# First-pair quads 0, 2, 3, 5 with one made ahead, and the residuals of the MLPs added by transfers

## The chip, the cores and the metric

The kernel runs on one core of one Trainium2 chip. The time is the device time of one execution in microseconds (us), median of three runs. It was 2813.29 us before the change (2812.1 to 2817.95).

## The reference, cut to what matters

Two transformer-like blocks follow each other on x, 256 tokens by 2048 channels, in float32. Each block has a normalisation, a wide input projection, three mixing branches with gates, an output projection added to x, and an MLP. The branches don't matter here. The MLP does:

```
x = x + merged @ w_out[l]
h2 = rmsnorm(x, norm2_g[l])
x = x + jnp.square(jax.nn.relu(h2 @ w_mlp_in[l])) @ w_mlp_out[l]      # 2048 -> 8192 -> 2048
```

The second block has the same with `w_o_2`, `w_up_2` and `w_down_2`; a last normalisation with `final_g` follows.

## The kernel before, in words

**Products in float32 from three products.** Every weight tile and every activation is split into a high part, rounded to float32r, and a low part, the rest. A product is high by high, high by low and low by high: three matmuls (`three`, L868). ScalarE makes the high part of a weight unit (`cut`, L1136) and VectorE the low one (L1609).

**Units.** The work of TensorE is one list of 2230 units. A plain unit is a weight tile of 256 rows by 512 columns, 512 KB, and both halves of 128 tokens: 12 matmuls. All engines walk the same list. SP loads unit u into one of four buffers when unit u - 4 has been split (L784). ScalarE and VectorE split unit u + 2 when they stand at u (AHEAD = 2), and the split buffers are four deep too. Beside the units, each engine has tasks, tied to a unit by `at(task, unit)`: an engine that stands at unit u first splits unit u + 2 and then does the tasks of u, in the order in which they were put there. An engine works strictly in that order, so a task that waits holds up all behind it.

**An MLP.** The 8192 hidden channels are made in eight groups of 1024. Group 0 is two plain blocks of eight units. Groups 1 to 7 are pairs: two blocks of 512 columns whose units alternate, eight quads of two units each. A quad is 2 x 2 tiles of weights by 2 x 2 tiles of activations, plainly 24 matmuls. For some quads seven products of sums of tiles stand in for eight (`pair_unit`, L873): 21 matmuls, for which VectorE makes three sums of weight tiles (L1622, L1624, L1626; four sums in all), ScalarE their high parts in two instructions (L1142, L1144) and VectorE their low parts in two (L1633). `SEVEN_I` (0, 1, 2, 3, 5, 6) are these quads in the six later pairs of each MLP, `FIRST_I` (1, 3, 5, 6) in the first. Quads 0 and 2 of the later pairs are made ahead: SP loads their weights once more into a tile of their own (L767), and the sums are made during the block before the pair (`ahead_sum`, `ahead_hi`, `ahead_lo`). The first pair has none made ahead. The sums of the activations (`x_sums`) are made during group 0.

**Second matrix.** After pair j come the four column blocks of group j - 1 with the second matrix, ("o1", j - 1, c) or ("o2", j - 1, c): four plain units each, 192 matmuls for the four. PSUM has two accumulator slots of two banks; block b uses slot b % 2. When a column block ends, VectorE adds it to X out of PSUM (`residual`, L2121) in the task ("ev", "o1") at the block's last unit, and that frees the slot. A pair takes both slots: its first quad needs the second one free in its second unit.

**Turning the hidden tile.** The hidden tile is transposed on VectorE (L2094), moved by four small transfers on SP's queue (L758), and split on ScalarE (L1408) and VectorE (L2115).

In the order of tasks at one unit, ("ev", "o1") stands ahead of `ahead_hi`, because it was put there first. GpSimd has hardly any work and issues no transfer.

Of the kernel before, what the change touches and what calls it, by code (L numbers as in the profile page):

```python
# [12 lines left out]
P = 128  # L13
# [32 lines left out]
def build(nc, a, out):  # L46
    ctx = ExitStack()

    def sem(name):
        return ctx.enter_context(nc.semaphore(name))  # L50
# [71 lines left out]

    NAMES = list(B)
    SEVEN_I = (0, 1, 2, 3, 5, 6)
    FIRST_I = (1, 3, 5, 6)
    MADE_AHEAD = (0, 2)
    SETS = ("T", "Y", "H", "T", "Y", "H")
    NI = len(SEVEN_I)
# [19 lines left out]
    for n in range(14):  # L148
        u0 = min(u for u in PAIR if PAIR[u][0] == n)
        js = FIRST_I if n % 7 == 0 else SEVEN_I  # L150
        ahead = () if n % 7 == 0 else MADE_AHEAD
        order = [i for i in js if i in ahead] + [i for i in js if i not in ahead]
        for k, i in enumerate(js):
            buf = ("TY"[k % 2] if n % 7 == 0 else SETS[k]) + str(n // 7 + 1)
            key = buf if buf[0] == "T" else (buf, n)
            rec = Seven(n, i, SEVEN_I.index(i), k == 0, k == len(js) - 1, i in ahead, buf, u0 + 2 * i, USED.get(key), made + order.index(i))
            USED[key] = u0 + 2 * i + 1
            SEVEN[u0 + 2 * i], SEVEN[u0 + 2 * i + 1] = (rec, 0), (rec, 1)
            if i in ahead:
                AHEAD_OF[n, ahead.index(i)] = rec  # L160
        PAIR_END[n] = u0 + 2 * js[-1] + 1
        made += len(js)
# [56 lines left out]
    zc_prod, cc_tap, vc_done = sem("cc_product"), sem("cc_tap"), sem("cc_out")  # L219
    pool_hi = sem("pool_hi")  # L220
    xs, xs_hi, xs_lo, diag, rsb = sem("x_sums"), sem("x_sums_hi"), sem("x_sums_lo"), sem("root_diagonal"), sem("root_rows")
    t_sum, t_hi, t_lo = sem("weight_sums"), sem("weight_sums_hi"), sem("weight_sums_lo")
    p1_out, mid, n_out, relu = sem("product1_out"), sem("product_sums"), sem("pair_out"), sem("pair_relu")
    x5_done, y_out, y_out_a = sem("final_gain"), sem("final_out"), sem("final_out_scalar")
# [24 lines left out]
    GB = [GBP[:, i, :] for i in range(2)]  # L249
    PR = GBP[:, :, :].rearrange("p a n -> p (a n)")[:, 0:768].rearrange("p (k j) -> p k j", j=32)  # L250
    JK = sb("JK", [P, 512])
    IDENT, TRI, ONES = CST[:, 0:P], CST[:, P:2 * P], CST[:, 2 * P:3 * P]
    AFTER, BOUND = CST[:, 3 * P:4 * P], CST[:, 4 * P:5 * P]
    ACC = ctx.enter_context(nc.psum_tensor("ACC", [P, 4, 512], F32))
# [164 lines left out]
    DG = JK[:, 0:3 * P]  # L419
    LOADED = {rec.q: k + 1 for k, rec in enumerate(AHEAD_OF.values())}  # L420

    def acc_bank(b, r):
        return ACC[:, 2 * (b % 2) + r, :]

# [149 lines left out]
                at(("ev", "o" + tag), last("o" + tag, j, c))  # L574
    AHEAD_LOAD = {}
    for n in range(14):
        if n % 7:
            h = min(u for u in PAIR if PAIR[u][0] == n)
            at("ahead_sum", h - 15)
            at("ahead_hi", h - 14)  # L580
            at("ahead_lo", h - 11, 2)
            at("ahead_sum", h - 6)
            at("ahead_hi", h - 5)
            at("ahead_lo", h - 4, 2)
            AHEAD_LOAD[h - 13], AHEAD_LOAD[h - 3] = AHEAD_OF[n, 0], AHEAD_OF[n, 1]
# [35 lines left out]
    def evicted(e, *name):  # L621
        b = B[name]
        e.wait_ge(acc[b % 2], b // 2 + 1)

    def multiplied(e, *name):
        e.wait_ge(mm, last(*name) + 1)
# [50 lines left out]
    def _(e):  # L677
# [11 lines left out]
        for u in range(NU):  # L689
# [2 lines left out]
                e.dma_start(dst, src).then_inc(landed, 16)  # L692
            for n, (g, c) in enumerate(GATES):
                if u == first(g, c) + 6:
                    if n >= 2:
                        evicted(e, *GATES[n - 2])
                    else:
                        e.wait_ge(c_done, 6)
                    e.dma_start(GB[n % 2], row(GBIAS[g][512 * c:512 * c + 512], 512)).then_inc(ld_gb[n % 2], 16)
# [60 lines left out]
            if u in AHEAD_LOAD:  # L760
                rec = AHEAD_LOAD[u]
                b0 = PAIR[rec.u][1]
                e.wait_ge(t_lo, 2 * rec.q)
                for m in range(2):
                    w, _, c0, n = plan[b0 + m]
                    rows = w[2 * rec.i * P:(2 * rec.i + 2) * P, c0:c0 + n].rearrange("(g t j) n -> j (g t) n", g=4, t=2)
                    e.dma_start(TR[rec.buf[1]][:, 2 * m:2 * m + 2, :], rows).then_inc(ld_sum, 16)  # L767
# [354 lines left out]
    def _(e):  # L1122
# [328 lines left out]
        def sums_split(tag):  # L1451
# [4 lines left out]
            e.activation(S4R[0], SX4[tag], ACT.Copy).then_inc(xs_hi, 1)  # L1456
            yield

        def x2_squares():
            for c in range(4):  # L1460
                evicted(e, "o1", 7, c)
                squares(X, R_2, c)
                yield
# [85 lines left out]
        def place_a():  # L1549
# [14 lines left out]
                 ("ev", "h1"): lambda: hidden_out("1", R_1), ("ev", "h2"): lambda: hidden_out("2", R_4),  # L1564
                 ("mid", "1"): lambda: product1_out("1"), ("mid", "2"): lambda: product1_out("2"),
                 ("xs_hi", "1"): lambda: sums_split("1"), ("xs_hi", "2"): lambda: sums_split("2"),
                 ("sq", "y"): y_squares,
                 "block1_end": block1_end, ("ev", "za"): za_out, "ua_put": lambda: put("ua", UA[:, :, 30:30 + L], ua_put),
                 "ln": norm, "lg": gain_back, ("ev", "zc"): zc_out, ("ev", "zb"): zb_out,
                 "pc_put": lambda: put("pc", PC[:, :, 2:2 + L], pc_put),  # L1570
# [29 lines left out]
    def _(e):  # L1600
# [603 lines left out]
                    yield  # L2204

        def o_out(tag):
            for j in range(8):
                for c in range(4):
                    if (tag, j, c) == ("2", 7, 3):
                        return  # L2210
                    residual(("o" + tag, j, c), c)
                    yield

        def y_gain():
            e.wait_ge(ld["fg2"], 16)
# [189 lines left out]
        for half in range(2):  # L2405
            x3, r5, t5 = X[:, half, 1536:2048], RS[R_5][:, half:half + 1], TOT[R_5][:, half:half + 1]
            e.wait_ge(last_half, half + 1)
            e.tensor_tensor(x3, x3, ACC[:, 2 * (B["o2", 7, 3] % 2) + half, :], ALU.add).then_inc(fin_x, 1)
            e.wait_ge(fin_x, half + 1)
            e.tensor_tensor(HB["2"][0][:, half, :], x3, FG2[:, 1536:2048], ALU.mult).then_inc(x5_done, 1)  # L2410
            e.wait_ge(squared, SQUARED[R_5] - 1 + half)
            e.tensor_reduce(t5, SUMS[R_5][:, half, :], mybir.AxisListType.X, ALU.add).then_inc(fin_root, 1)
            e.wait_ge(fin_root, 3 * half + 1)
            e.tensor_scalar(t5, t5, 1.0 / D, EPS, ALU.mult, ALU.add).then_inc(fin_root, 1)
            e.wait_ge(fin_sqrt, half + 1)
            e.reciprocal(r5, t5).then_inc(fin_root, 1)
            e.wait_ge(fin_root, 3 * half + 3)
            e.wait_ge(x5_done, 7 + half)
            for cs in (slice(0, 1024), slice(1024, 1536)):
                y = X[:, half, cs]  # L2420
                e.tensor_scalar(y, y, r5, None, ALU.mult, ALU.bypass).then_inc(y_out, 1)
# [3 lines left out]
    @blk.gpsimd  # L2425
    def _(e):

        def stream(u, front):
            front()

        def gm_tril():
            e.wait_ge(ld["gw"], 32)
            e.affine_select(out=WS, in_=WS, compare_op=ALU.is_ge, fill=0.0, base=0, pattern=[[0, 8], [1, P]],
                            channel_multiplier=-1).then_inc(ws_done, 1)
            yield

        def pad():
            multiplied(e, "o1", 7, 3)
            e.wait_ge(turn_lo, 2 * TN["x2", 3] + 2)
            e.memset(UA[:, :, 0:30], 0.0).then_inc(pads, 1)  # L2440
            e.memset(PC[:, :, 0:2], 0.0).then_inc(pads, 1)
            yield

        tasks = {"gm_tril": gm_tril, "block1_end": pad}
        run(e, stream, tasks)

    ctx.close()
# [55 lines left out]
```

## Time and profile before

| what | value |
|---|---|
| median of three runs | 2813.29 us |
| the profiled execution | 2816.21 us, its span 2814.5 us |
| TensorE busy | 2791.1 us, 99% |
| VectorE busy | 2227.4 us, 79% |
| ScalarE busy | 1489.3 us, 53% |
| granted TensorE clock | 0.999 |
| residual additions (L2121) | 71, 86.3 us |
| bytes moved | 615.42 MB |

The first MLP lies from about 820 to 1500 us of the span, the second from about 2127 to the end. TensorE is busy nearly all the time, so a change shows only where TensorE waits.

### The profile page before, as it was taken

The numbers are of one execution on the slowest core, as the hardware profiler recorded it, in microseconds if no ns is written. First come the engines' busy times: TensorE is split into PE (matmuls) and PEld (weight loads), VectorE is DVE, ScalarE is ACT, GpSimd is POOL, SyncE is SP. The second block draws the span as 40 slices with busy tenths as digits, with TensorE's granted clock in tenths as the row PEclk, the third lists the DMA queues.
The fourth block names the chain that finished last, engine by engine and source line by source line (L and its number), as shares of the span: only waits on it lengthen the run. The fifth ranks groups of instructions, "written<-read, shape, count | busy, mean of one in ns | idle before, by whom it ended". The sixth has DMA issues, their size and how long they took to land.

```text
span 2814.5 us, 33866 instructions
## 1 busy us (share of the span) xinstructions
PE 2791.1 (99%) x13102; PEld 2300.4 (82%) x13102; DVE 2227.4 (79%) x2487; ACT 1489.3 (53%) x1674; POOL 2.0 (0%) x7
## 2 busy tenths in 40 slices
PE   9999999999999999999999999999999999999998
PEld 7888878888887888888888888888888788888887
DVE  6697855556778999999967678877667999999986
ACT  6644446544455555555556444444455555555654
POOL 0000000000000000000000000000000000000000
PEclk9999999999999999999999999999999999999999
DMA  9576656666866677767677767667676767677774
GB/s 313 160 222 201 204 160 211 195 195 198 257 210 212 219 235 243 245 212 239 223 243 218 223 199 215 200 206 224 209 219 208 243 215 239 219 242 226 246 233 166
DMA packets 371808, 615.42 MB, mean 219 GB/s; under 512 B 22976, under 2 KB 96320, under 8 KB 371008
## 3 DMA queue, kind: packets, MB, share of 16 engines
q1 hardware_dynamic: 371216, 612.94, 68.8%
q8 instruction: 103, 1.69, 0.2%
q14 instruction: 57, 0.47, 0.1%
q10 hardware_dynamic: 432, 0.32, 0.0%
HBM read 575.69 MB, written 2.10 MB: 205 GB/s over the span
## 4 chain that ended last, share of the span: by engine, by line
PE 83%; DVE 8%; DMA 5%; ACT 2%; issue 2%; SPq 1%; DVEq 0%; ACTq 0%
PE ACC L864 67%; PE TB L870 8%; PE ACC L870 6%; DVE WL L1609 2%; DMA RAW<-in_w_mlp_in_dram 2%; DMA RAW<-in_w_up_dram 2%; DMA RAW<-in_w_down_dram 1%; DVE FG L1622 1%; ACT WH L1136 1%; DVE FG L1624 1%; DVE FG L1626 1%; DVE X L2121 0%; DVE HT L2094 0%; SPq L758 0%; DVE TWL L1633 0%
## 5 line engine op out<-in xcount | busy, mean ns | idle before, releaser
L1136 ACT ACTIVATE WH<-RAW 128x1024 fp32r<-128x1024 f32 (+1 forms) x1023 | 1027.8, 1020 | 1016.4 <-PE ACC L864 619.1
L1609 DVE TENSOR_TENSOR WL<-RAW,WH 128x1024 fp32r<-128x1024 f32 (+1 forms) x1023 | 1185.6, 1172 | 405.5 <-ACT WH L1136 402.5
L864 PE MATMUL ACC<-WH,XTH 128*128 128x512 f32 (+1 forms) x1692 | 658.1, 389 | 0.4 <-DVE XTL L1683 0.4
L864 PE MATMUL ACC<-WL,XTH 128*128 128x512 f32 (+1 forms) x1692 | 655.1, 387 | 0.0
L864 PE MATMUL ACC<-WH,XTL 128*128 128x512 f32 (+1 forms) x1692 | 655.1, 387 | 0.0
L864 PEld LDWEIGHTS ACC<-WH,XTH 128*128 128x128 f32 x1692 | 317.8, 188 | 66.8 <-DVE XTL L1683 0.8
L864 PEld LDWEIGHTS ACC<-WH,XTL 128*128 128x128 f32 x1692 | 317.7, 188 | 65.1
L864 PEld LDWEIGHTS ACC<-WL,XTH 128*128 128x128 f32 x1692 | 317.8, 188 | 63.6
L864 PE MATMUL ACC<-WH,YAH 128*128 128x512 f32 x864 | 336.4, 389 | 0.0
L864 PE MATMUL ACC<-WL,YAH 128*128 128x512 f32 x864 | 336.1, 389 | 0.0
L864 PE MATMUL ACC<-WH,YAL 128*128 128x512 f32 x864 | 336.1, 389 | 0.0
L864 PE MATMUL ACC<-WH,YBH 128*128 128x512 f32 x512 | 199.2, 389 | 0.0
L864 PE MATMUL ACC<-WL,YBH 128*128 128x512 f32 x512 | 199.2, 389 | 0.0
L864 PE MATMUL ACC<-WH,YBL 128*128 128x512 f32 x512 | 199.2, 389 | 0.0
L864 PEld LDWEIGHTS ACC<-WH,YAH 128*128 128x128 f32 x864 | 162.2, 188 | 34.3 <-DVE WL L1609 0.6
L864 PEld LDWEIGHTS ACC<-WH,YAL 128*128 128x128 f32 x864 | 162.2, 188 | 33.7
L864 PEld LDWEIGHTS ACC<-WL,YAH 128*128 128x128 f32 x864 | 162.2, 188 | 33.5
L2121 DVE TENSOR_TENSOR X<-X,ACC 128x1024 f32<-128x1024 f32 x71 | 86.3, 1215 | 60.2 <-PE ACC L864 60.2
L870 PE MATMUL TB<-WH,XBH 128*128 128x512 f32 x336 | 130.8, 389 | 0.0
L870 PE MATMUL TB<-WL,XBH 128*128 128x512 f32 x336 | 130.7, 389 | 0.0
L870 PE MATMUL TB<-WH,XBL 128*128 128x512 f32 x336 | 130.7, 389 | 0.0
L864 PEld LDWEIGHTS ACC<-WH,YBH 128*128 128x128 f32 x512 | 96.1, 188 | 20.2 <-DVE WL L1609 0.2
(383 smaller groups left out, 3146.6 us busy)
## 6 DMA issues: line engine op xcount, KB each, us to landing
RAW<-in_w_in_dram SPq DMA_DIRECT2D x255, 512.0 KB, 4.5
RAW<-in_w_mlp_out_dram SPq DMA_DIRECT2D x128, 512.0 KB, 5.0
RAW<-in_w_down_dram SPq DMA_DIRECT2D x128, 512.0 KB, 5.1
RAW<-in_w_mlp_in_dram SPq DMA_DIRECT2D x116, 512.0 KB, 4.6
RAW<-in_w_up_dram SPq DMA_DIRECT2D x116, 512.0 KB, 4.5
RAW<-in_w_gate_dram SPq DMA_DIRECT2D x96, 512.0 KB, 4.5
YT<-HT SPq DMA_DIRECT2D x208, 128.0 KB, 3.2
RAW<-in_w_branch_dram SPq DMA_DIRECT2D x48, 512.0 KB, 4.1
```

The costliest lines, as they stand in the source:

```text
L864: ins = e.matmul(ACC[:, 2 * (b % 2) + half, 0:n], p[:, k, xs], q[:, t, 0:n], start=(k == 0 and m == 0), stop=(k == nk - 1 and m == 2))
L870: ins = e.matmul(dst, p, q, start=(start and m == 0), stop=(stop and m == 2))
L1136: e.activation(WH[u % NSPL][:, ts, 0:n], RAW[u % NRAW][:, ts, 0:n], ACT.Copy).then_inc(hi, 1)
L1609: e.tensor_tensor(l, r, h, ALU.subtract).then_inc(lo, 1)
L1622: e.tensor_tensor(tr[:, T1:T3 + 1:T3 - T1, :], b12_22, b11_12, ALU.subtract).then_inc(t_sum, 1)
L1624: e.tensor_tensor(tr[:, T2, :], b22, tr[:, T1, :], ALU.subtract).then_inc(t_sum, 1)
L1626: e.tensor_tensor(tr[:, T4, :], b21, tr[:, T2, :], ALU.subtract).then_inc(t_sum, 1)
L2121: e.tensor_tensor(xv, xv, ACC[:, 2 * (b % 2):2 * (b % 2) + 2, :], ALU.add).then_inc(acc[b % 2], 1)
```

## The change

The first pair of each MLP takes quads 0, 2, 3 and 5 in place of 1, 3, 5 and 6, and its quad 0 is made ahead, in the last part of the projection before. The additions to X of groups 0 to 6 of the second matrix leave VectorE: ScalarE copies the column block out of PSUM into one of two buffers, which frees the accumulator slot, and GpSimd issues a transfer that adds the buffer to X in SBUF. Those of group 7 stay on VectorE and wait for the last transfer to the same columns. In the diff, `o_copy` is ScalarE's task, `o_out` VectorE's and `o_add` GpSimd's.

```diff
-    FIRST_I = (1, 3, 5, 6)
+    FIRST_I = (0, 2, 3, 5)
...
-        ahead = () if n % 7 == 0 else MADE_AHEAD
+        ahead = MADE_AHEAD[:1] if n % 7 == 0 else MADE_AHEAD
...
+    RB = [GBP, sb("RB", [P, 2, 512])]
...
+        if n % 7 == 0:
+            at("ahead_sum", h - 29)
+            at("ahead_hi", h - 28)
+            at("ahead_lo", h - 27)
+            at("ahead_lo", h - 25)
+            AHEAD_LOAD[h - 32] = AHEAD_OF[n, 0]
...
+        def o_copy(tag):
+            for j in range(7):
+                for c in range(4):
+                    n, b = RN["o" + tag, j, c], B["o" + tag, j, c]
+                    if n >= 2:
+                        e.wait_ge(res_added[n % 2], 16 * (n // 2))
+                    multiplied(e, "o" + tag, j, c)
+                    e.activation(RB[n % 2], ACC[:, 2 * (b % 2):2 * (b % 2) + 2, :], ACT.Copy).then_inc(acc[b % 2], 1)
+                    yield
...
         def o_out(tag):
-            for j in range(8):
-                for c in range(4):
-                    if (tag, j, c) == ("2", 7, 3):
-                        return
-                    residual(("o" + tag, j, c), c)
-                    yield
+            for _ in range(28):
+                yield
+            for c in range(4):
+                if (tag, c) == ("2", 3):
+                    return
+                added(e, "o" + tag, 6, c)
+                residual(("o" + tag, 7, c), c)
+                yield
...
+        def o_add(tag):
+            for j in range(7):
+                for c in range(4):
+                    n = RN["o" + tag, j, c]
+                    evicted(e, "o" + tag, j, c)
+                    e.dma_start(X[:, :, 512 * c:512 * c + 512], RB[n % 2], accum_op=ALU.add).then_inc(res_added[n % 2], 16)
+                    yield
```

## Rows read from the trace of the kernel before

**Rows 1.** The page: the span, and busy time of each engine.
```profile
span 2814.5 us, 33866 instructions
PE 2791.1 (99%) x13102; PEld 2300.4 (82%) x13102; DVE 2227.4 (79%) x2487; ACT 1489.3 (53%) x1674; POOL 2.0 (0%) x7
```
**Rows 2.** Waits of TensorE: total us, times, longest us.
```profile
PE ACC L870 <- DVE WL L1609: 7.6, 10, 1.7
PE ACC L870 <- DVE X L2121: 3.5, 5, 1.6
```
**Rows 3.** The chain of waits in order of time: start us, us, what.
```profile
910.86 32.85 PE ACC L864 x144
...
1079.52 32.65 PE ACC L864 x144
...
1412.89 275.88 PE ACC L864 x1260
...
2216.75 43.75 PE ACC L864 x192
...
2720.00 87.05 PE ACC L864 x384
```
**Rows 4.** By stretch: busy us (instructions) per engine, granted clock, DMA share, GB/s.
```profile
1079.50:1123.10 43.60, 43.60 (x194) 36.08 (x193) 39.45 (x39) 25.51 (x26) 0.00 (x0) 1.00 0.79 252
1123.10:1162.80 39.70, 39.65 (x175) 32.52 (x174) 37.26 (x41) 22.70 (x25) 0.00 (x0) 1.00 0.64 213
1102.00:1104.00 2.00, 2.00 (x10) 1.66 (x9) 2.00 (x3) 0.00 (x0) 0.00 (x0) 1.00 0.73 196
1104.00:1110.00 6.00, 6.00 (x28) 4.95 (x28) 5.28 (x6) 2.96 (x3) 0.00 (x0) 1.00 1.05 398
```
**Rows 5.** The residual additions in the page: busy us, mean ns of one.
```profile
L2121 DVE TENSOR_TENSOR X<-X,ACC 128x1024 f32<-128x1024 f32 x71 | 86.3, 1215 | 60.2 <-PE ACC L864 60.2
```
**Rows 6.** ScalarE's timeline around a second-matrix block and its pair: start us, us, instruction.
```profile
1110.25 1.07 ACT L1136 ACTIVATE WH<-RAW 128x1024 fp32r<-128x1024 f32 x1 [2.47 <-DMA RAW<-in_w_mlp_out_dram]
1111.37 1.06 ACT L1142 ACTIVATE TWH<-FG 128x1024 fp32r<-128x1024 f32 x1
...
1113.28 2.94 ACT L1136 ACTIVATE WH<-RAW 128x1024 fp32r<-128x1024 f32 x3
...
1157.50 0.60 ACT L1447 ACTIVATE HB<-ACC 128x512 f32<-128x512 f32 x1 [3.19 <-PE TB L870]
```
**Rows 7.** VectorE's timeline in the same stretch.
```profile
1114.36 1.23 DVE L1609 TENSOR_TENSOR WL<-RAW,WH 128x1024 fp32r<-128x1024 f32 x1
...
1121.94 1.23 DVE L1622 TENSOR_TENSOR FG<-RAW 128x1024 f32<-128x1024 f32 x1 [1.22 <-DMA RAW<-in_w_mlp_in_dram]
...
1125.67 1.82 DVE L1609 TENSOR_TENSOR WL<-RAW,WH 128x1024 fp32r<-128x1024 f32 x2
...
1150.96 1.82 DVE L1609 TENSOR_TENSOR WL<-RAW,WH 128x1024 fp32r<-128x1024 f32 x2
```
**Rows 8.** SP's issues in the same stretch.
```profile
1100.68 1.26 SPq L767 DMA_DIRECT2D FG<-in_w_mlp_in_dram  x2
1101.98 5.79 SPq L784 DMA_DIRECT2D RAW<-in_w_mlp_out_dram  x3
```
**Rows 9.** TensorE's timeline: starts of both first pairs, and a wait in one.
```profile
864.53 0.39 PE L870 MATMUL TB<-WH,XBH 128*128 128x512 f32 x1
...
900.36 0.50 PE L870 MATMUL ACC<-WH,XTH 128*128 128x512 f32 x1 [1.67 <-DVE WL L1609]
...
2170.95 0.39 PE L870 MATMUL TB<-WH,XBH 128*128 128x512 f32 x1
```
**Rows 10.** VectorE's timeline in the projection before and in the first pair.
```profile
787.76 1.22 DVE L1609 TENSOR_TENSOR WL<-RAW,WH 128x1024 fp32r<-128x1024 f32 x1 [3.28 <-ACT WH L1136]
...
864.89 1.22 DVE L1609 TENSOR_TENSOR WL<-RAW,WH 128x1024 fp32r<-128x1024 f32 x1
...
879.56 1.30 DVE L2094 STREAM_TRANSPOSE HT<-HB 128x512 f32<-128x512 f32 x2
```

More of the change, by code:

```diff
@@ L221, in build @@
     xs, xs_hi, xs_lo, diag, rsb = sem("x_sums"), sem("x_sums_hi"), sem("x_sums_lo"), sem("root_diagonal"), sem("root_rows")
+    res_added = [sem(f"residual_added{i}") for i in range(2)]
     t_sum, t_hi, t_lo = sem("weight_sums"), sem("weight_sums_hi"), sem("weight_sums_lo")
@@ L420, in build @@
     LOADED = {rec.q: k + 1 for k, rec in enumerate(AHEAD_OF.values())}
+    RN = {("o" + tag, j, c): 28 * n + 4 * j + c for n, tag in enumerate("12") for j in range(7) for c in range(4)}
     def acc_bank(b, r):
@@ L576, in build @@
     for n in range(14):
-        if n % 7:
-            h = min(u for u in PAIR if PAIR[u][0] == n)
+        h = min(u for u in PAIR if PAIR[u][0] == n)
+        if n % 7 == 0:
[4 more added lines that the diff above has]
+            AHEAD_LOAD[h - 32] = AHEAD_OF[n, 0]
+        else:
             at("ahead_sum", h - 15)
@@ L623, in evicted, with added @@
         e.wait_ge(acc[b % 2], b // 2 + 1)
+    def added(e, *name):
+        n = RN[name]
+        e.wait_ge(res_added[n % 2], 16 * (n // 2) + 16)
     def multiplied(e, *name):
@@ L694, in _ @@
                 if u == first(g, c) + 6:
+                    if (g, c) == ("g2b", 0):
+                        added(e, "o1", 6, 2)
                     if n >= 2:
@@ L762, in _ @@
                 b0 = PAIR[rec.u][1]
+                if rec.n % 7 == 0:
+                    e.wait_ge(turned, TN["m" + rec.buf[1], 3] + 1)
                 e.wait_ge(t_lo, 2 * rec.q)
@@ L1566, in _ @@
                  ("xs_hi", "1"): lambda: sums_split("1"), ("xs_hi", "2"): lambda: sums_split("2"),
-                 ("sq", "y"): y_squares,
+                 ("sq", "y"): y_squares, ("ev", "o1"): lambda: o_copy("1"), ("ev", "o2"): lambda: o_copy("2"),
                  "block1_end": block1_end, ("ev", "za"): za_out, "ua_put": lambda: put("ua", UA[:, :, 30:30 + L], ua_put),
@@ L2407, in _ @@
             e.wait_ge(last_half, half + 1)
+            added(e, "o2", 6, 3)
             e.tensor_tensor(x3, x3, ACC[:, 2 * (B["o2", 7, 3] % 2) + half, :], ALU.add).then_inc(fin_x, 1)
@@ L2442, in pad @@
             yield
-        tasks = {"gm_tril": gm_tril, "block1_end": pad}
+        def o_add(tag):
[5 more added lines that the diff above has]
+                    yield
+        tasks = {"gm_tril": gm_tril, "block1_end": pad, ("ev", "o1"): lambda: o_add("1"), ("ev", "o2"): lambda: o_add("2")}
         run(e, stream, tasks)
```

## The prediction

> **What bounds the kernel now.** I read the page first. TensorE is busy for 2791.1 of 2814.5 us [rows 1], so nothing that frees another engine helps unless TensorE waits for it. The number of matmuls stays: the first pair of each MLP keeps four quads at 21 matmuls (seven products of three) and four at 24. So the change can only move waiting time of TensorE, and the granted clock is 1.00 in all stretches read [rows 4].
>
> The view of waits names two releasers that belong to the MLPs: VectorE's splits of the weights (L1609, 7.6 us) and the residual additions (L2121, 3.5 us) [rows 2]. It misses the slower restarts, so I take the whole loss from start times in the chain of waits [rows 3]. 384 matmuls take 87.05 us, 0.2267 each. A later pair has 6 x 21 + 2 x 24 = 174 matmuls, a block of products of the second matrix 192, together 82.96 us; six of them 497.8. The first MLP takes 1412.89 - 910.86 = 502.0 us for six, the second 2720.00 - 2216.75 = 503.3: lost 4.3 and 5.5, together 9.8 us over 12 pairs. A first pair has 180 matmuls, 40.8 us; it takes 910.86 - 864.53 = 46.3 us in the first MLP and 2216.75 - 2170.95 = 45.8 in the second [rows 3, 9]: 5.5 and 5.0 lost. **All that the change can win back is 9.8 + 10.5 = 20.3 us.**
>
> The third view is the table by stretch: in the 43.6 us of a second-matrix block the DMA engines are 0.79 busy, in the pair behind it 0.64; between 1104 and 1110 they are full (1.05, 398 GB/s) [rows 4]. Then the timelines of ScalarE, VectorE and SP over the same block [rows 6 to 8].
>
> **Part 1, residuals.** 56 of the 71 additions (28 per MLP) leave VectorE, 1.215 us each [rows 5], four per pair: 4.9 us of 83, off an engine 39.45 of 43.6 us busy in such a block [rows 4]. ScalarE gets 56 copies of 128x1024 out of PSUM. No such copy is in the trace; half of it takes 0.60 us [rows 6], so between 1.0 and 1.2, I take 1.05. It is 25.51 us busy in the block, so load is no matter; order is. GpSimd gets 56 transfers. Nothing waits for one for ten microseconds: a buffer comes back two blocks (21.8 us) later.
>
> *What goes.* At a pair's start TensorE waits until the last column block's bank is free. VectorE comes late there, because it first makes the sums of quad 1, which wait for a weight load (1121.94, then the addition, then the splits at 1125.67) [rows 7]. The copy on ScalarE is ready 1.1 us behind the block's end, and TensorE needs the bank 12 matmuls, 2.7 us, in: this wait goes, 3.5 us by the view, about 5 with restarts.
>
> *What comes instead: ScalarE's order.* The copy waits for the block's end, and everything behind it on ScalarE waits too. Let h be the first unit of the next pair. In column block 2, which ends with unit h-5, that is the pair of rounded copies of the sums made ahead (today 1111.37 to 1113.28, before the block's end) and the next weight unit [rows 6]. The block ends 144 matmuls after 1079.52, at 1112.2. Copy to 1113.3, two sum copies at 0.97 to 1115.2, unit h-2 to 1116.2, VectorE's split 1.14 to 1117.4 (today 1115.5, its start at 1114.36 [rows 7]). TensorE needs it 24 matmuls behind the block's end, at 1117.6. So it just holds, but all weight buffers come free 1.9 us later. The load for quad 1 is issued at about 1119.7 in place of 1117.8, lands 4.1 us later at 1123.8 (today 1121.9), and the sums start there. Behind them stands no addition any more, so quad 1's splits end at 1128.1 in place of 1127.4: 0.7 later. The rest of the pair is a chain of load, sums and splits; today quad 6's split starts at 1150.96 and ends at 1152.1 [rows 7], TensorE needs it 129 matmuls in (five quads of 21 and one of 24), at 1152.3. 0.7 later costs about 0.4 with the restart. Over 12 pairs that is 4.8 us, against the 9.8 of today, if the transfers cost nothing.
>
> *The transfers.* SP issues the 1 MB of the second sums made ahead at 1100.68 and the next weights at 1101.98 [rows 8]; ScalarE gets those, unit h-3, only at 1110.25, after waiting 2.47 us [rows 6], with the engines full in between [rows 4]. Column block 1 ends at 1101.3; its transfer starts at about 1103.5, in this burst. No accumulating transfer is in the trace. From below it costs nothing (if it fits between the others) or 512 KB at 400 GB/s, 1.3 us; but both the copy and X have to be read, so 1 MB, 2.6 us. I take 2.6, since the addition can't be made without the second read, and keep 0 and 5.2 as ends. Some 0.4 of the 2.6 fit ahead of the burst (share 0.73 up to 1104 [rows 4]); the weights come at 1112.4 in place of 1110.2 and ScalarE's row becomes: unit h-3 to 1113.4, copy to 1114.5, sums to 1116.4, unit h-2 to 1117.4, VectorE to 1118.6. TensorE stands 1.0 us. Low part and split of h-1 end at 1120.9, the load for quad 1 lands at 1125.0, 3.1 later than today; less the addition of 1.1 the splits are 2.0 later, quad 6 is ready at 1154.1 against a need of 1153.3, 0.8 late. The transfer of block 3 (from about 1126) can meet the load of quad 3 and make that 2.0. With restarts a pair loses 2.0 to 3.2 us; I take 2.0, since the load of quad 3 is issued only at 1129 and that transfer is then almost done: 24 us in place of 9.8, **+14.2**. By 1.3 us for a transfer the same steps give 1.2 per pair, 14.4: +4.6.
>
> The Trainium skill (Collectives: The Full Stack, The bandwidth ceiling) says of the adding unit in the DMA path that it costs by its two source reads, half the rate of a copy, and not by the addition; this trace has no such transfer. By that rule the sum is the one with 2.6. The skill (DMA: Bandwidth & Descriptors, Issuing engines are not separate DMA queues) also has GpSimd's transfers interleave with SP's on the same 16 engines; by that rule a burst like the one at 1104 has no free place.
>
> **Part 2, first pairs.** Quad 0's sums move into the projection before. SP is moved past 1 MB more there, VectorE past three sums and two low parts (2.6 and 2.3 us), ScalarE past two copies. VectorE's idle gap behind unit 269's split is 3.28 us and TensorE's next need is a whole block ahead [rows 10], so TensorE does not see it; if the cover were gone it would cost up to 4.9 per MLP. In the pair, quad 0 then costs VectorE only its splits. But quads 2 and 3 stand next to each other, as 5 and 6 do today, and those cost TensorE 1.67 us and a restart at 900.36 [rows 9]: VectorE needs 2.6 for sums, 1.8 for splits and 2.3 for low parts, 6.7 against 4.76. Between quads 2 and 3 stand also a transpose (1.30) and a split of the hidden tile (about 1.2). Replayed from the split of unit 297 at 864.89 [rows 10]: load for quad 2 lands at 871.0, sums to 873.6, splits and low parts to 877.7, sums of quad 3 to 880.3, transpose to 881.5, split to 882.7. Quad 2 ends on TensorE at 879.6: 3.1 us of waiting, then 0.4 and 0.5 for the low parts, 4.4 with restarts. Quad 5 stands alone and fits. Lost 4.4 in place of 5.5 and 5.0: **-1.7**. Bounds: -6 if the load for quad 3 lets VectorE run ahead, +4 if both meet worse.
>
> **Sum.** +14.2 - 1.7 = +12.5. Against the profiled execution (span 2814.5, 2816.2 us with what lies around it) 2828.7; the median of the runs is 2813.3, 2.9 lower, so the same step gives 2825.8. I say 2825.
>
> **Rivals.** *Near nothing.* The transfer costs 1.3 us or less and finds gaps: 4.8 to 14.4 in place of 9.8, and -1.7: -7 to +3, 2806 to 2816. For it: the mean share of 0.79 leaves 9 us in each block, four transfers want 5.2 to 10.4. Against: the wait of 2.47 in the full stretch.
> *Faster.* VectorE is the real bound of the MLPs, and 4.9 us per pair less lets it run ahead far enough that its loads are asked for earlier; then ScalarE's copy is waited for with everything behind already done. 6 to 9 of the 9.8 and 2 to 4 of the 10.5 come back: -8 to -13, say 2803. It decides at block 2: unit h-3 has to be split before the block ends, and the load for quad 1 to land before the pair starts. For it: both releasers are VectorE, and it is back to back from 1122 on. Against: four ScalarE steps then follow the block's end, which no free VectorE shortens.
> *Much slower.* The addition in the DMA path is slower than reading, 5.2 us or more: 35 us busy and 21 more in 43.6. About 3 us more per pair than forecast: 2860.
> *No effect of the quads*, or worse by the pile between 2 and 3: +3 on any of these.
>
> **Numbers.** Slower by the forecast's step 0.43, much slower 0.07, near nothing 0.27, faster 0.23. 0.2% is 5.6 us, about what a measurement of this kernel can tell from no change. Near nothing lies within it almost whole: faster 0.24, same 0.28, slower 0.48. The forecast's own range is 2817 to 2842; to hold 8 in 10 it goes from 2804 to 2842.
>
> **What would show it.** L2121 x15, and no wait of TensorE for it in the MLPs; 56 copies of about 1.05 us on ScalarE. In a block, weights of unit h-3 landing 2 us later behind the block's start and TensorE waiting for L1609 at unit h-2: forecast right. The share of the DMA engines in the block at 0.90 or more; at 0.85 and no wait at h-2, near nothing. In the first pair one wait of about 3 us at quad 3 and none at quad 6. Wrong altogether if the 12 pairs lose less than 9.8 us.

## The result, and the profile after

| kernel | median us (range) | profiled execution | span |
|---|---|---|---|
| before | 2814.23 (2812.1 to 2817.95) | 2816.21 | 2814.5 |
| after | 2866.61 (2864.97 to 2868.37) | 2865.67 | 2864.0 |

Four runs each. After stands to before as 1.0183, 95% interval 1.0167 to 1.0199: 52 us slower, where the forecast said 12 and its range ended at 2842. The granted clock is 0.998 (0.999 before), 0.996 in the other three runs, so the clock is a small part of it: in the twelve blocks and pairs 21 matmuls lie 0.43 us apart in place of 0.23, behind three long waits (last section), about 4 us.

The page first: its span line, engine line and the queue lines (packets, MB, share of 16 engines).
```profile
span 2864.0 us, 33986 instructions
PE 2806.3 (98%) x13102; PEld 2302.3 (80%) x13102; DVE 2168.2 (76%) x2431; ACT 1534.1 (54%) x1730; POOL 70.1 (2%) x63
...
q1 hardware_dynamic: 372048, 614.51, 67.5%
q0 software_dynamic: 15232, 29.36, 5.8%
```
Against [rows 1] TensorE has the same 13,102 matmuls (in 1024 units; the 2230 given for the list above is wrong). VectorE is 59 us less busy for 56 additions fewer (68 us of them). The second queue is new: 56 transfers hold all 16 engines for 5.8% of 2864.0, 166 us, 2.97 us each.

TensorE's waits (total us, times, longest us) answer to [rows 2].
```profile
PE ACC L882 <- DVE WL L1637: 26.9, 21, 2.3
PE ACC L888 <- DVE WL L1637: 18.9, 25, 2.3
```
The wait for the additions (L2121 in [rows 2]) is gone. L888 is the pair's matmul, where before lost 7.6 us. L882 is the plain matmul, in the second-matrix blocks, where before had no such wait at all. That is the new thing, and it is the larger one.

The chain in order of time, for the stretches without a wait.
```profile
1436.96 275.93 PE ACC L882 x1260
...
2769.34 87.19 PE ACC L882 x384
```
384 matmuls still take 0.2271 us each, and the 1260 behind the first MLP's last pairs are as dense as in [rows 3]. Everything is lost between.

The start times of TensorE, read over the whole trace, give the mean length of each kind of stretch. This table carries most of what follows. The floor is the number of matmuls times 0.2267. "Stretch ahead" is the last stretch ahead of a first pair, 144 matmuls from the first to the pair's first; there is one per MLP.

| kernel | block (192) | pair (174) | first pairs | stretch ahead |
|---|---|---|---|---|
| floor | 43.52 | 39.44 | 40.8 | 32.6 |
| before | 43.56 | 40.22 | 46.17, 45.63 | 33.33 |
| after | 46.71 | 41.28 | 44.71, 44.74 | 34.04 |

Twelve blocks lose 12 x 3.15 = 37.8 us against before, twelve pairs 12 x 1.065 = 12.8. The first pairs give back 2.4 and the stretches ahead of them take 1.4. Sum +49.6; the spans differ by 49.5.

The same block as in [rows 4], and the pair behind it, by stretch (us; busy us and instructions of TensorE, its weight loads, VectorE, ScalarE and GpSimd; granted clock; DMA share; GB/s).
```profile
1085.83:1132.10 46.27, 44.15 (x194) 35.88 (x192) 35.41 (x35) 26.93 (x28) 3.64 (x3) 1.00 0.90 267
1132.10:1173.35 41.25, 40.02 (x175) 32.50 (x174) 36.83 (x40) 24.34 (x27) 1.22 (x1) 1.00 0.72 223
...
1110.00:1119.00 9.00, 9.00 (x42) 7.44 (x41) 6.17 (x6) 3.73 (x4) 0.53 (x1) 1.00 1.01 303
```
DMA share 0.90 in the block, 0.79 before. The full stretch is 9 us long instead of 6, and at the same full share it moves 303 GB/s where [rows 4] has 398: the engines are as busy and deliver less.

SP's issues ahead of it, and GpSimd's.
```profile
1102.25 4.30 SPq L774 DMA_DIRECT2D YT<-HT  x4
1106.59 1.28 SPq L802 DMA_DIRECT2D RAW<-in_w_mlp_out_dram  x2
1107.92 1.27 SPq L785 DMA_DIRECT2D FG<-in_w_mlp_in_dram  x2
1109.23 5.83 SPq L802 DMA_DIRECT2D RAW<-in_w_mlp_out_dram  x3
```
```profile
1099.16 1.21 POOL L2480 DMA_DIRECT2D X<-GBP  x1 [50.96 <-ACT GBP L1484]
1109.31 1.22 POOL L2480 DMA_DIRECT2D X<-RB  x1 [8.94 <-ACT RB L1484]
1122.69 1.21 POOL L2480 DMA_DIRECT2D X<-GBP  x1 [12.17 <-ACT GBP L1484]
```
Count from the block's start, 1085.83. Block 0's transfer is issued 13.3 us in and block 1's 23.5 us in, in the same moment as the weights of unit h-3 (23.4; h is the first unit of the next pair). In before those were issued 22.6 us in (1101.98 [rows 8] less the block's first matmul at 1079.35): SP is already 0.8 late, and here the reader sees why: the four copies YT<-HT, which shift the hidden tile, take SP 4.30 us. In before they took 2.63.

ScalarE, then VectorE, at the block's end, and TensorE.
```profile
1120.36 1.06 ACT L1154 ACTIVATE WH<-RAW 128x1024 fp32r<-128x1024 f32 x1 [5.29 <-DMA RAW<-in_w_mlp_out_dram]
1121.33 1.00 ACT L1484 ACTIVATE GBP<-ACC 128x1024 f32<-128x1024 f32 x1
1122.23 1.04 ACT L1160 ACTIVATE TWH<-FG 128x1024 fp32r<-128x1024 f32 x1
1123.18 1.05 ACT L1162 ACTIVATE TWH<-FG 128x1024 fp32r<-128x1024 f32 x1
1124.13 3.46 ACT L1154 ACTIVATE WH<-RAW 128x1024 fp32r<-128x1024 f32 x4
```
```profile
1125.20 1.23 DVE L1637 TENSOR_TENSOR WL<-RAW,WH 128x1024 fp32r<-128x1024 f32 x1 [2.52 <-ACT WH L1154]
```
```profile
1122.73 0.50 PE L882 MATMUL ACC<-WH,YAH 128*128 128x512 f32 x1 [1.38 <-DVE WL L1637]
...
1126.48 0.50 PE L882 MATMUL ACC<-WH,YAH 128*128 128x512 f32 x1 [0.74 <-DVE WL L1637]
```
The row at 1120.36 answers to the one at 1110.25 in [rows 6]. ScalarE waited 5.29 us for the weights in place of 2.47. They come 34.5 us into the block, in before 30.9 (1110.25 less 1079.35). TensorE needs unit h-3 156 matmuls in, at 35.4. From ScalarE's start on it to TensorE's lie 2.37 us here (1120.36 to 1122.73), so 33.0 us in is the limit for unit h-3. 34.5 is 1.5 past it: TensorE stands 1.38 us and restarts slowly. Then comes ScalarE's order as forecast, the copy of block 2 and the two sum copies, and unit h-2 is cut from 1124.13 and split at 1125.20: TensorE stands once more, 0.74.

Unit h-2 has a limit of its own, and it comes first. TensorE needs it 168 matmuls in, at 38.1, and with ScalarE's order it starts 6.12 us behind ScalarE's start on unit h-3 (1120.36 to 1126.48). So from 32.0 us in every later arrival of the weights of h-3 costs TensorE time: up to 33.0 at unit h-2, beyond it at unit h-3 too.

### The profile page after: what moved, and what is told of

Same layout as the page of the kernel before. It is cut to its first block, busy times and chain, and to the rows that moved or that the text cites. A ratio compares the mean times of both kernels' runs of the same rounds, so it can differ in the third digit from the quotient of the medians.

```text
span 2864.0 us, 33986 instructions
## 1 busy us (share of the span) xinstructions
PE 2806.3 (98%) x13102; PEld 2302.3 (80%) x13102; DVE 2168.2 (76%) x2431; ACT 1534.1 (54%) x1730; POOL 70.1 (2%) x63
## 4 chain that ended last, share of the span: by engine, by line
PE 65%; DVE 15%; DMA 11%; issue 4%; ACT 4%; SPq 1%; DVEq 0%; ACTq 0%
PE ACC L882 59%; DVE WL L1637 5%; DMA RAW<-in_w_up_dram 3%; DMA RAW<-in_w_mlp_in_dram 3%; DVE FG L1650 3%; PE TB L888 3%; DVE FG L1652 2%; PE ACC L888 1%; DMA FG<-in_w_mlp_in_dram 1%; DMA FG<-in_w_up_dram 1%; ACT WH L1154 1%; DVE FG L1654 1%; DVE HB L2230 1%; DVE TSL L1661 1%; ACT HB L1455 1%
## 5 line engine op out<-in xcount | busy, mean ns | idle before, releaser
L882 PE MATMUL ACC<-WH,XTH 128*128 128x512 f32 (+1 forms) x1692 | 658.2, 389 | 0.0
L882 PE MATMUL ACC<-WL,XTH 128*128 128x512 f32 (+1 forms) x1692 | 655.2, 387 | 0.0
L882 PE MATMUL ACC<-WH,XTL 128*128 128x512 f32 (+1 forms) x1692 | 655.0, 387 | 0.0
L882 PEld LDWEIGHTS ACC<-WH,XTH 128*128 128x128 f32 x1692 | 317.7, 188 | 65.8 <-DVE WL L1637 0.4
L882 PEld LDWEIGHTS ACC<-WH,XTL 128*128 128x128 f32 x1692 | 317.7, 188 | 64.9
L882 PEld LDWEIGHTS ACC<-WL,XTH 128*128 128x128 f32 x1692 | 317.8, 188 | 64.1
L882 PE MATMUL ACC<-WH,YAH 128*128 128x512 f32 x864 | 338.2, 391 | 13.0 <-DVE WL L1637 13.0
L882 PE MATMUL ACC<-WH,YAL 128*128 128x512 f32 x864 | 336.9, 390 | 0.0
L882 PE MATMUL ACC<-WL,YAH 128*128 128x512 f32 x864 | 336.8, 390 | 0.0
L882 PE MATMUL ACC<-WH,YBH 128*128 128x512 f32 x512 | 201.9, 394 | 13.9 <-DVE WL L1637 13.9
L882 PEld LDWEIGHTS ACC<-WH,YAH 128*128 128x128 f32 x864 | 162.6, 188 | 51.1 <-DVE WL L1637 17.6
L882 PE MATMUL ACC<-WL,YBH 128*128 128x512 f32 x512 | 200.5, 392 | 0.0
L882 PE MATMUL ACC<-WH,YBL 128*128 128x512 f32 x512 | 200.5, 392 | 0.0
L882 PEld LDWEIGHTS ACC<-WH,YAL 128*128 128x128 f32 x864 | 162.5, 188 | 34.2
L882 PEld LDWEIGHTS ACC<-WL,YAH 128*128 128x128 f32 x864 | 162.6, 188 | 33.3
L888 PE MATMUL TB<-WH,XBH 128*128 128x512 f32 x336 | 130.9, 390 | 0.0
L888 PE MATMUL TB<-WH,XBL 128*128 128x512 f32 x336 | 130.8, 389 | 0.0
L888 PE MATMUL TB<-WL,XBH 128*128 128x512 f32 x336 | 130.8, 389 | 0.0
L882 PEld LDWEIGHTS ACC<-WH,YBH 128*128 128x128 f32 x512 | 96.9, 189 | 38.7 <-DVE WL L1637 18.7
L882 PEld LDWEIGHTS ACC<-WH,YBL 128*128 128x128 f32 x512 | 96.8, 189 | 20.5
```

The source lines that it names most:

```text
L882: ins = e.matmul(ACC[:, 2 * (b % 2) + half, 0:n], p[:, k, xs], q[:, t, 0:n], start=(k == 0 and m == 0), stop=(k == nk - 1 and m == 2))
L888: ins = e.matmul(dst, p, q, start=(start and m == 0), stop=(stop and m == 2))
```

## The experiments

Each was run beside the kernel before, which stood at 2815.3 in the runs up to e8, at 2816.4 in e9 to e12 and at 2815.8 in e13 to e15; so a difference between two kernels of different groups is uncertain by 1 us more. "Block" and "pair" are the means of the table above. Where residual additions are missing, that is the whole of what a kernel leaves out: they are not on VectorE and in no transfer.

**Which half of the change?** `e1_quads_only` has the change of the quads and nothing of the residuals; `e2_copies_no_transfer` is the whole change without GpSimd's transfers.

```diff
 # e2, against after
                     evicted(e, "o" + tag, j, c)
-                    e.dma_start(X[:, :, 512 * c:512 * c + 512], RB[n % 2], accum_op=ALU.add).then_inc(res_added[n % 2], 16)
```

> The kernel before with the first pairs' quads 0, 2, 3, 5 and quad 0 made ahead; the residuals stay on VectorE. Every theory of the residuals leaves this alone. By the two traces the first pairs went from 46.2 and 45.6 us to 44.7 and 44.8 and the group 0 stretch ahead of each became 0.7 longer: -1 us in all, 2813, not to be told from no change. If the slowdown comes from the quads instead (loads asked for in the projection), over 2840.

> The kernel after without the 56 transfers: groups 0 to 6 of the second matrices are copied out of PSUM by ScalarE and never added to X (that part of the result is left out). Theory A, the transfers' time on full DMA engines makes weights late: nearly all of the 52 us is gone and the waits for the accumulator slot stay gone, 2805 to 2812. Theory B, the copy holds up ScalarE (sum copies and next weight unit behind the block's end): 30 us or more of the 52 stay, 2845 or more. Mixed: 2820 to 2840.

e1: 2816.38, ratio 1.0008 [0.9999, 1.0016]. e2: 2823.16, 1.003 [1.0018, 1.0042]. e2 falls into its mixed range. The quads are worth nothing. Copies, order and freed VectorE together cost 8 us. So 43 of the 52 us are the transfers. e2's block takes 43.62 and its pair 40.80, so the 3 us lost in each block are the transfers' alone. e1's first pairs take 44.87 and 45.19 and its stretches ahead 34.04: what the pairs win, the stretches lose.

**Is it the second read, or any transfer?** Both kernels are before, with 56 transfers of the same size from a buffer that VectorE no longer touches into a spare tile, issued by GpSimd behind each addition. Nothing waits for them but the next of their kind.

```diff
+                    evicted(e, "o" + tag, j, c)
+                    e.dma_start(SPARE, GBP, accum_op=ALU.add).then_inc(spare_done, 16)   # e3
+                    e.dma_start(SPARE, GBP).then_inc(spare_done, 16)                     # e4
```

> The kernel before, residuals on VectorE as they were, and beside them 56 adding transfers of the same size from GpSimd at the same places, into a spare tile nobody reads. Theory A: weights of unit h-3 land 2.5 to 3 us later, but ScalarE's order is the old one: 1.5 to 3 us per pair, 2832 to 2850. Theory B: within 6 us of 2814.

> As the run with the adding transfers beside, but they copy and don't add. If the second read is what an adding transfer costs, its share of the DMA engines halves (from 2.97 us of all 16 per transfer to about 1.5) and less than half of that run's loss stays. If the loss comes from GpSimd's issuing (1.21 us each) or from a second queue as such, the time is that of the adding ones within 3 us.

e3: 2911.57, 1.0344 [1.033, 1.0359]. e4: 2845.7, 1.0109 [1.0094, 1.0125]. The queue line of e3, then of e4, and e3's waits of TensorE (total, times, longest):
```profile
q0 software_dynamic: 8064, 29.36, 6.3%
```
```profile
q0 software_dynamic: 8064, 29.36, 2.9%
```
```profile
PE ACC L868 <- DVE WL L1613: 31.6, 15, 3.3
PE ACC L874 <- DVE WL L1613: 27.5, 27, 2.6
PE ACC L874 <- DVE X L2125: 19.6, 12, 2.6
```
Same bytes, same packets: 2909.5 x 0.063 / 56 = 3.27 us of all engines with the addition, 2843.3 x 0.029 / 56 = 1.47 without. Adding 3.27 us of full engines 56 times (183 us) made the kernel 96 us slower. No forecast had that: the higher one ended at 2850. L868 is the plain matmul: the wait in the blocks is there again. And the wait for X, 3.5 in before, grows to 19.6, since VectorE's addition stands in its order behind the sums of quad 1, which wait for a load that is now late. Some 15 us of the 96 are clock: in its blocks and pairs 73 matmuls lie 0.43 us apart in place of 0.23.

The plain transfers of e4 cost 30 us, less than half of 96, as forecast for the second read. But 30 is not little, and nearly all of it is one wait, the one that the change removes:
```profile
PE ACC L874 <- DVE X L2125: 20.8, 12, 2.5
```
At that matmul of the pair, the 13th, e4's twelve pairs lose 22.7 us with the restarts. Where VectorE still frees the accumulator slot, a plain transfer is enough to hold it up.

**When, and in which order?** Against after: `e5_block1_transfer_later` holds block 1's transfer until block 2 is multiplied, out of the full stretch; `e6_sum_copies_first` and `e9_no_transfer_sum_copies_first` put the two sum copies ahead of block 2's copy on ScalarE, with the transfers and without.

```diff
+                    if c == 1:                          # e5, ahead of dma_start
+                        multiplied(e, "o" + tag, j, 2)
-            at("ahead_hi", h - 5)                       # e6 and e9
+            behind[h - 5].insert(0, "ahead_hi")
```

> The kernel after, only the transfer of column block 1 is issued when block 2 has ended, behind the burst of the second sums' load and the next weights. Theory place (the loss is that one transfer meeting the full stretch): TensorE's waits at units h-3 and h-2 go, the 12 blocks fall from 46.3 to 47.7 us back to 43.6 or 44, 2830 to 2838. Theory sum (any 3 us of the 16 engines cost the same, wherever they lie): the time stays at 2860 to 2870, since the same transfers run, two of them now together.

> The kernel after, only ScalarE makes the two high copies of the second sums ahead of the copy out of PSUM at the end of column block 2, not behind it. Without transfers ScalarE's order cost 8 us against before. If that order works the same way beside the transfers, unit h-2 comes up to 1.9 us sooner and the wait there (about 0.9 with restart) goes: 2848 to 2858. Rival: ScalarE waits for the weights of h-3 anyway and the sums are late too (VectorE waits for their load), so nothing can go first: within 3 us of 2866.

> The kernel of the run without transfers (additions of groups 0 to 6 left out), with ScalarE's high copies of the second sums ahead of the copy out of PSUM of block 2. That kernel was 8 us slower than before, a pair 40.8 us in place of 40.2. If those 8 us are ScalarE's order at block 2 (late unit h-2, late buffers, late load of quad 1): a pair falls to 39.9 or less, 2808 to 2813. Rival, the copy of block 3 at the pair's start is what costs: stays at 2820 to 2824.

| kernel | us | ratio [95%] | block | pair |
|---|---|---|---|---|
| e5 | 2861.75 | 1.0165 [1.0149, 1.018] | 43.76 | 43.53 |
| e6 | 2867.99 | 1.0183 [1.0169, 1.0197] | 46.88 | 41.23 |
| e9 | 2811.99 | 0.9984 [0.9975, 0.9992] | 43.54 | 39.88 |

e5 settles what the block waits for: with one transfer moved, the block is back at 43.76. It wins almost nothing, though, because the pair takes over what the block gave, 43.53 in place of 41.28. So its time is the one forecast by "sum" and its place the one forecast by "place". Its waits, and TensorE's timeline in one pair:
```profile
PE ACC L888 <- DVE WL L1637: 38.5, 24, 2.8
...
PE ACC L882 <- DVE WL L1637: 0.7, 2, 0.5
```
```profile
1145.81 0.50 PE L888 MATMUL ACC<-WH,XTH 128*128 128x512 f32 x1 [2.73 <-DVE WL L1637]
...
1147.57 0.63 PE L888 MATMUL TB<-WH,XTH 128*128 128x512 f32 x1
1147.99 0.63 PE L888 MATMUL TB<-WL,XTH 128*128 128x512 f32 x1
```
e6 moves nothing: behind late weights the order of the copies is not what is last. e9 against e2 is 11 us: without the transfers the order is worth that, all of it in the pair (39.88 against 40.80). The prediction's step "ScalarE's order" is real: 11 us with one order of the copies more than with the other.

**The useful part alone.** `e7_copy3_vector_adds_late` and `e8_copy3_transfer_adds` have before's quads and change only block 3 of groups 0 to 5, the one whose bank TensorE waits for: ScalarE copies it out. In e7 VectorE adds the copy to X three units later; in e8 a transfer adds it.

```diff
+                at(("copy3", tag), last("o" + tag, j, 3))
+                at(("late3", tag), last("o" + tag, j, 3) + 3)
+        def copy3(tag):                                  # ScalarE
+                e.activation(GBP, ACC[:, 2 * (b % 2):2 * (b % 2) + 2, :], ACT.Copy).then_inc(acc[b % 2], 1)
+        def late3(tag):                                  # e7, VectorE
+                e.tensor_tensor(X[:, :, 1536:2048], X[:, :, 1536:2048], GBP, ALU.add).then_inc(late, 1)
+        def add3(tag):                                   # e8, GpSimd
+                e.dma_start(X[:, :, 1536:2048], GBP, accum_op=ALU.add).then_inc(late, 16)
```

> The kernel before with one change: column block 3 of groups 0 to 5 is copied out of PSUM by ScalarE, which frees the slot, and VectorE adds the copy to X three units later, where it waits for a load. No transfer. The view of waits gives 3.5 us for the slot, about 5 with restarts: 2808 to 2811. Rival: the copy holds ScalarE at the start of the pair as in the run without transfers (+8 there with four copies): 2814 to 2818.

> As the run before this one, but GpSimd's adding transfer takes the place of VectorE's late addition: 12 transfers, all at the start of a pair, where the engines are 0.64 busy. Theory place: a transfer there meets only the loads of quads 1 and 3 and costs 0 to 0.8 us per pair: 2808 to 2822. Theory sum: 12/56 of the 44 us that the transfers cost in the kernel after, about 9: 2817 to 2822, and no less than 2815.

e7: 2809.0, 0.9975 [0.9965, 0.9985]. e8: 2823.2, 1.0027 [1.0018, 1.0036]. e7 is the fastest complete kernel of this study, faster than before by 0.25%: its block takes 43.55, its pair 39.84 (0.4 from the floor). Its largest wait in the MLPs, and ScalarE where the copy frees the bank:
```profile
PE ACC L877 <- DVE WL L1625: 7.1, 11, 1.7
```
```profile
1119.71 1.03 ACT L1472 ACTIVATE GBP<-ACC 128x1024 f32<-128x1024 f32 x1 [4.81 <-PE ACC L871]
```
The wait for X is gone and nothing is in its place. In e8 twelve transfers, where the mean share is lowest (0.64 in the pair [rows 4]), cost 14.2 us against e7: 1.2 us each, 12 of the 14 in the pairs (40.83). That is above both of its forecasts, and a low mean share is not the best place: in e12 below the same kind of transfer costs next to nothing in the fuller block.

**Which transfer?** All are after, with transfers of some column blocks only (e14: all four, without the addition in them).

```diff
+                    if c == 0:                          # e10; c == 1: e11; c == 2: e12; c == 3: e15; c in (0, 1): e13
                     e.dma_start(X[:, :, 512 * c:512 * c + 512], RB[n % 2], accum_op=ALU.add).then_inc(res_added[n % 2], 16)
```

> The kernel after with all copies, but only the 14 transfers of column block 0 (the additions of blocks 1 to 3 of groups 0 to 6 left out). Without any transfer 2823, with all four 2867. Place (only those in the full stretch cost): block 0's ends before it, 2823 to 2826. Sum (each the same): 11 more, 2834.

> The same with the transfers of column block 1 alone, those that meet the full stretch. Place: most of the 44 us, 2845 to 2860, with TensorE's waits at units h-3 and h-2. Sum: 2834. If the waits at h-3 need the backlog of block 0's transfer too: 2823 to 2832 and no such wait.

> The same with the transfers of column block 2 alone; they run from about 1.5 us behind that block's end, where the engines are half free, but ahead of the loads of quads 0 and 1. Place: 2823 to 2826. Sum: 2834. In the run with block 1's transfer moved here the pairs grew by 2.2 us: if a load of quad 1 is what it meets, 2830 to 2840 and the wait at quads 1 or 3.

> All copies and the transfers of column blocks 0 and 1 together (the additions of blocks 2 and 3 of groups 0 to 6 left out). Alone they cost 3.7 and 12.7 us over the 2823 without transfers. If the prices add, 2839.5 and a block of 45.1 us. If block 0's transfer leaves a backlog that reaches into the full stretch, they do not add: 2846 to 2858, a block of 46 us or more, which would be most of what the four cost together beyond the sum of their single prices.

> The kernel after with transfers that overwrite X in place of adding to it (the additions of groups 0 to 6 left out, the transfers and copies stay): one read less per transfer, everything else the same. If the second read carries the cost: queue 0 falls from 5.8% of the engines to about 2.9%, and less than half of the 44 us stay, 2830 to 2842. If the queue, the packets or GpSimd's issue carry it: 2855 to 2867.

> As the runs of one block each, for block 3 (its transfer starts 1.1 us into the pair). Against VectorE's late addition it cost 14 us for 12 transfers in another kernel: if it meets the loads of quads 1 and 3 here too, 2832 to 2838; if ScalarE's order has already made those loads late enough to miss it, 2823 to 2828.

The last column is where in the block ScalarE starts on unit h-3, that is, when its weights have come: the mean of the twelve blocks of each kernel. The limits worked out above are 32.0 (unit h-2) and 33.0 (unit h-3). "Over e2" is the plain difference of the medians, uncertain by 1 to 2 us.

| kernel | us | ratio [95%] | over e2 | block | pair | h-3 at |
|---|---|---|---|---|---|---|
| e2, none | 2823.16 | 1.003 [1.0018, 1.0042] | 0 | 43.62 | 40.80 | 30.4 |
| e14, all, plain | 2826.01 | 1.0038 [1.0023, 1.0052] | 2.8 | 43.78 | 40.71 | 32.0 |
| e12, block 2 | 2824.05 | 1.0027 [1.0018, 1.0037] | 0.9 | 43.68 | 40.67 | 30.7 |
| e10, block 0 | 2826.81 | 1.0035 [1.0023, 1.0047] | 3.7 | 43.94 | 40.93 | 32.2 |
| e15, block 3 | 2828.46 | 1.0045 [1.003, 1.006] | 5.3 | 43.65 | 41.12 | 30.7 |
| e11, block 1 | 2835.87 | 1.007 [1.0055, 1.0085] | 12.7 | 44.73 | 40.76 | 33.0 |
| e13, blocks 0 and 1 | 2859.25 | 1.0154 [1.0139, 1.0169] | 36.1 | 46.81 | 40.48 | 34.9 |
| after, all | 2866.61 | 1.0183 [1.0167, 1.0199] | 43.5 | 46.71 | 41.28 | 34.8 |

"Each costs the same" (11 us) falls with e10, e12 and e15; that e11 lies near its 2834 is chance. Single prices add up to 22.6 us, the four together cost 43.5. Most of the excess is in blocks 0 and 1: alone 3.7 and 12.7, together 36.1, beyond the 2846 to 2858 forecast for a backlog. Read the last column for it. Block 0's transfer moves the weights by 1.8 us, to just past the first limit, and a block pays 0.3 us for it. Block 1's moves them by 2.6, to 1.0 past that limit, and a block pays 1.1, most of it at unit h-2 as the prediction had it (0.8; 0.2 at h-3). Together they move them by 4.5, to 2.9 past it, and a block pays 3.2. So what a block pays is, within 0.3 us, what the arrival is past 32.0: delays add, prices do not, because the first 1.6 us of delay are free.

How block 0's transfer reaches weights that are asked for nine microseconds later is in SP's timeline. In e10, then in e11, which lacks that transfer:
```profile
1094.52 4.71 SPq L774 DMA_DIRECT2D YT<-HT  x4
1099.28 1.27 SPq L802 DMA_DIRECT2D RAW<-in_w_mlp_out_dram  x2
1100.59 1.27 SPq L785 DMA_DIRECT2D FG<-in_w_mlp_in_dram  x2
```
```profile
1096.05 2.65 SPq L774 DMA_DIRECT2D YT<-HT  x4
```
Issued 1.6 us behind the end of GpSimd's issue for block 0 (1091.71 to 1092.92 in e10), four issues of SP take 4.71 us instead of 2.65. SP then issues the sums' load later in its block than in e2 (22.2 us in against 20.9 in the mean of twelve), and the weights behind it. The twelve blocks of the other kernels bear it out. In after, e5, e6, e10 and e13, which have this adding transfer, the four issues take 4.1 to 5.0 us in all 60 blocks. Without it (before, e2, e11, e12, e15) they take 2.6 to 3.4 in nearly all, with a single block of 3.9 to 4.7 in four of the five kernels. e14's plain transfer at the same place leaves them at 2.6 to 3.2. It is not the addition alone, though: e4's plain transfer, issued 1.7 us later in the block (15.0 in place of 13.3 us in) and so closer to SP's four issues, makes them 3.0 to 4.1. Why an issue takes longer there no run shows.

e14 lies below its forecast of 2830 to 2842. One thing differs in it beside the addition: a plain transfer to X has 144 packets, an adding one 272, and holds GpSimd 0.72 us in place of 1.21. e3 and e4, with 144 packets each, differ by 66 us all the same, so the second read costs much by itself; how the 41 us between after and e14 divide no run shows.

Left open: the 7 us that the transfers of blocks 2 and 3 add once 0 and 1 are there (43.5 less 36.1). Alone they cost 0.9 and 5.3, 6.2 together, which the medians can't tell from 7; but the pairs grow by 0.80 us from e13 to after and by 0.19 from e2 in e12 and e15 together, so the agreement may be chance, and no run had three of the four. And no run of a transfer was tried with SP's order changed, the weights of h-3 ahead of the sums' load.

## Why the prediction was wrong

**The bound and the loss of before**: right. 20.3 us was all that could come back, and the best kernel found gets back 6.3 (e7).

**The slot wait goes**: right in after and e7. Against before, e7 wins 4.6 us in the twelve pairs by it (0.38 each), against 3.5 to 5 in the forecast.

**ScalarE's order at 0.4 us per pair**: a term of the sum that was mis-sized. e2, with no transfer at all, has block and pair 1.46 us over the floor, 1.06 more than forecast: 12.7 us. The waits are where the forecast put them, late in the pair: at quad 6 all twelve pairs of e2 stand, 0.87 us each (10.4 in all) in place of 0.4, and five stand at quad 1 as well (1.8 in all). e9, with only the order of the sum copies changed, has 0.46 over the floor. So the place was right and the size was not. The step that "just holds", unit h-2 at the end of block 2, did hold: in none of e2's twelve blocks does TensorE stand there. What went wrong is the replay of the pair, which carried one lateness of 0.7 us, of quad 1, through a pair that otherwise kept its distances.

**Freed VectorE**: the rival "VectorE is the real bound" fell. e9 frees it of all 56 additions and takes 2811.99; e7 frees it of none and takes 2809.0.

**A transfer of 2.6 us**: nearly right, 2.97 by the page of the profile. The Trainium skill (Collectives: The Full Stack, The bandwidth ceiling) has an addition in the DMA path cost by its two source reads, at half a copy's rate. The runs agree and go slightly past it: 3.27 against 1.47 us beside before, and in the change's own place the transfers cost 43.5 us adding and 2.8 plain (e14, with half the packets).

**"Only block 1's transfer meets the burst"**: this is the step that failed. The forecast let one transfer delay the weights of h-3, to 33.05 us into the block (1112.4 less 1079.35), and TensorE by 1.0 us. e11, which has just that transfer, measures 33.0 and a block 1.1 longer than e2's: for one transfer the step is right to a tenth. But it gave the transfer of block 0 no effect, since the share was below one there and nothing waited for it. It goes with slower issues of SP itself, the weights of h-3 come 1.9 us later still (34.9 in e13), and as the first limit of 32.0 is passed already, the block pays all of that. Over e2, block and pair lose 3.57 us more in after; the forecast had 1.6 for the transfers (2.0 less 0.4). 12 x 1.97 = 24 us, and with the 12.7 of the order these are the 36 to 37 that block and pair take beyond the forecast; the spans say 37 (49.5 less 12.5). The working took a mean share below one as room, and did not follow a delayed queue into the next full stretch.

**Blocks 2 and 3**: "can make that 2.0 to 3.2" was right in kind. Block 3's transfer alone costs 5.3 us, 4 of them in the pairs.

**The first pairs**: -1.7 forecast, -2.4 measured, the second in part by luck. The first pair comes ahead of all that the experiments change, so its other runs count too: with before's quads (before, e3, e4, e7, e8) it takes 44.8 to 46.2 us, 45.55 in the mean, with the new ones (the other twelve) 44.1 to 45.8, 44.95 in the mean, so -1.2 for the two. The one wait at quad 3 is there, 1.9 us long at 881.95 in place of 3.1 (2.3 in the second MLP), and there is none at quad 6; quad 5, which was to fit, has one of 0.5 and 0.2. But a wait at the end of the stretch ahead, +0.7 per MLP, was not foreseen:
```profile
864.83 0.47 PE L888 MATMUL ACC<-WH,XTH 128*128 128x512 f32 x1 [0.54 <-DVE XTL L2203]
```
VectorE, moved past quad 0's sums, gives the last low part of the activations late. The two cancel: e1 is at 1.0008.

**The rivals**: "much slower" came near the time with 2860, by luck and for the wrong cause: it wanted an addition slower than reading, 5.2 us a transfer, and it is 2.97. "Near nothing" fell with e11 and e8: only block 2's transfer (e12) finds the gaps that the mean share leaves.

**The signs**: L2121 (now L2149) x15, copies of 1.0 us, a share of 0.90, and the wait at h-2 are all there. The wait at h-3 itself, 1.38 us and the larger, was not in the list; the weights were 1.5 us later in this block than the forecast had them.

## What to carry to other kernels

- Before giving load to a queue that looks idle, ask of each transfer what is issued or in flight while it lasts, on every queue, and carry the delay on to the next full stretch. Give the consumer's limit as a time, and add up all delays against it: two that cost 4 and 13 us alone cost 36 together.
- Where an engine waits for a buffer, free the buffer with the least work that does it (e7: one copy in four) and leave the rest of the work where it is. The full change, which took all four additions off an engine that was not last, ended 52 us slower than before.
- For a step that "just holds", work out from which arrival on it fails. Here it held in all of e2's blocks, the first 1.6 us of delay of the weights cost nothing, and each 1 us beyond them cost a block 1 us.

## What the runs showed of the hardware

- A transfer of 512 KB from SBUF to SBUF that adds takes 2.97 (after) to 3.27 us (e3) of all 16 engines, a plain one of the same size 1.47 (e4). From issue to landing the first took 6.8 us in the middle (5.2 to 10.7) in after; beside before it took 6.6, the plain one 4.7. GpSimd was held 1.21 us by each issue in after and 0.72 by the plain ones of e14, and in the spare-tile kernels 0.86 with the addition and 0.53 without.
- While an adding transfer of GpSimd was in flight, four issues of SP took 4.1 to 5.0 us in place of 2.6 (60 blocks of five kernels); beside e14's plain ones 2.6 to 3.2, beside e4's, which were issued closer to them, 3.0 to 4.1.
- In e5, after a wait of 2.73 us, TensorE ran at a granted clock of 0.50, its lower level of 1.2 GHz. The stretch, with its columns as above:
```profile
1147.50:1150.10 2.60, 2.60 (x7) 1.99 (x6) 2.60 (x3) 0.63 (x2) 0.00 (x0) 0.50 0.94 349
```
The first slow matmul started 1.3 us behind the restart (1147.14), and seven lay 0.43 us apart in place of 0.23: 1.4 us on top of the wait. After had three such stretches in its blocks and pairs, behind waits of 1.88, 2.29 and 2.31 us, and none behind others of up to 2.26; the one behind 2.31 us:
```profile
1387.00:1390.00 3.00, 3.00 (x9) 2.27 (x9) 1.16 (x2) 3.00 (x4) 0.54 (x1) 0.54 0.73 156
```
